# Computing the first three input-projection chunks side by side while x arrives, in a hybrid decoder layer

## The chip, the cores and the metric

One NeuronCore of one Trainium2 chip runs the whole layer as a single program. The metric is device time in microseconds for one execution; the kernel before took 484.26 us (median of 3 runs, 484.12 to 484.92).

## The reference, cut to what matters

```python
h = rmsnorm(x, norm_g)                       # x: 512 tokens x 1024
proj = jnp.einsum('bsd,de->bse', h, w_in)    # 1024 -> 4896 columns, split into 16 parts
# A: RG-LRU on lru_u:  conv (4 taps) -> xc;  r, i = sigmoid(xc @ wa + ba), sigmoid(xc @ wx + bx)
#    a = exp(-8 r softplus(-lam));  h_t = a h_{t-1} + sqrt(1 - a^2) i xc;  y = h * silu(z)
# B: native sparse attention (compressed, selected, window) with sigmoid gates, * silu(z)
# C: forgetting attention with a cumulative log-forget bias, * silu(z)
return x + jnp.einsum('bse,ed->bsd', concat(y_lru, y_nsa, y_fox), w_out)
```

Everything is float32. The mean of squares of x over the 1024 features gives one scale per token (rstd); the kernel multiplies it in after the projection, so the matmuls can start before it is known.

## The kernel before

**Precision.** Each float32 operand of the projections is split into a high part (a copy rounded to fp32r, made on ScalarE) and a low part (operand minus high, made on VectorE). A product is three matmuls: high x high, high x low, low x high.

**Tiling.** x arrives transposed as 8 slices of 128 features x 512 tokens (`x_raw`, 256 KB each), and becomes `xh` and `xl`. The input weights are cut into 39 chunks of 128 output columns (512 KB each); `CHUNKS` gives their order: u0 to u3 (chunks 0 to 3), fg (4), kc, vc, ks, kw (5 to 8), nq0 to nq3 (9 to 12), vn0 and vn1 (13, 14), zl0 to zl3 (15 to 18), and then the rest. A chunk lands in one of three `raw` slots; `split` (line 497, ScalarE) writes `wh`, `split_low` (line 763, VectorE) writes `wl`. `project(c)` (line 1074, TensorE) runs 8 x 3 matmuls of 128x512 (lines 1110 to 1112) into one of three PSUM banks. It waits for `wl_ready` of its chunk and, from the fourth chunk on, for the bank: the chunk three places back must have been read.

**The start.** SyncE issues x0, the channel constants, x1 to x3, w0, x4 to x7, w1, w2, constants, the compression weights, w3. ScalarE makes `xh` of each slice (line 634) and puts `split(0)` behind slice 4, `split(1)` behind slice 7, `split(2)` behind the square root (line 639). VectorE squares slices 0, 2, 4, 6, 7 (line 977) and makes `xl` of each (line 981); GpSimd squares slices 1, 3, 5 (line 462). TensorE sums all eight squares over partitions with a matrix of ones into MEAN (line 1253, a float32 matmul that the trace shows as two records), and only then begins `project(0)`. The scale is the square root on ScalarE and the reciprocal on VectorE (line 1004).

**The loop over chunks.** No scheduler: the order on each engine is the order of this code, and each engine's queue is served in order. In its turn c each engine does:
- TensorE: `project(c)`, then for the chunk before, if it is a u, the two gate matmuls `gates_of(c - 1)` (lines 1129 and 1130). So the gates of u3 stand behind chunk 4. The mean of squares of a normalised key or query chunk (line 1121) stands in the middle of the next chunk.
- ScalarE: `split(c + 3)`, `before(c)` (first conv tap of u, line 522; square of ks, line 534), then `after(c - 1)`: two sigmoids and a tanh of the gates (lines 544 to 547). At kc it also does a block that needs the tanh of all four u chunks (lines 661 to 669): four square roots, two small ones for the forget gate, four pairs of Ln and Exp, and only behind it `split(9)`.
- VectorE: `before(c)`: the eviction of chunk c times the scale (line 745) and three conv taps of u (line 756); `after(c - 1)`; pieces of the LRU tail at vc, ks, kw, nq0 and vn (lines 827 to 832, `TAIL_AT`), which need ScalarE's block; and last `split_low(c + 3)`.
- At vc, VectorE also needs the forget gate's logarithm from ScalarE's block (lines 798 and 799).

At zl0, TensorE's transpose (line 1165) needs the compressed-attention probabilities, which VectorE makes (line 897) after all that stands ahead of them in its queue.

Of the kernel before, what the change touches and what calls it, by code (L numbers as in the profile page):

```python
# [18 lines left out]
F32 = mybir.dt.float32  # L19
F32R = mybir.dt.float32r  # L20
BF16 = mybir.dt.bfloat16
ACT = mybir.ActivationFunctionType
ALU = mybir.AluOpType
AX = mybir.AxisListType

P = 128
SEQ, D = 512, 1024
HD = 64
KT = D // P
# [24 lines left out]
NSA_END = AT["zl", 3] + 1  # L54
# [29 lines left out]
TAIL_AT = (AT["vc", 0], AT["vc", 0], AT["ks", 0], AT["ks", 0], AT["kw", 0], AT["nq", 0], AT["vn", 0], AT["vn", 0])  # L84
OUT_ORDER = (2, 0, 3, 1)
STACK_LAG = 6
POOL_SQUARES = (1, 3, 5)
VECTOR_SQUARES = tuple(k for k in range(KT) if k not in POOL_SQUARES)

GAIN = {"ks": "ks_g", "kw": "kw_g", "nq": "nq_g", "fq": "fq_g", "fk": "fk_g"}  # L90

# [1 line left out]
def program(nc, xT, x_tok, w_in, w_out, chan, const, lru_w, cmp_w, out):  # L93
    ctx = ExitStack()
    with ctx:
        def sem(name):
            return ctx.enter_context(nc.semaphore(name))
# [98 lines left out]
        raw_loaded = [sem(f"raw_loaded{i}") for i in range(RAW)]  # L196
        wh_ready, wl_ready, w_used = sem("wh_ready"), sem("wl_ready"), sem("w_used")
        xh_ready, xl_ready, x_sq = sem("xh_ready"), sem("xl_ready"), sem("x_sq")
        x_sq_pool, x_sq_used = sem("x_sq_pool"), sem("x_sq_used")
        std_ready = sem("std_ready")  # L200
        rstd_ready, rstd_T, rcol_ready = sem("rstd_ready"), sem("rstd_T"), sem("rcol_ready")
        small_consts = sem("small_consts")
# [55 lines left out]

            return sum(0 if CHUNKS[x][0] in ("nq", "fq") else 4 for x in NORMED[:c])

        def pool_square(k):
            return (sq, work, std)[POOL_SQUARES.index(k)][:, :]

        def half_of(s):
            return slice(s * HD, (s + 1) * HD)
# [117 lines left out]
        @block.sync  # L383
        def _(sp):
            def load_w(c):
                if c >= N_STREAM:
                    return
                if c >= RAW:
                    sp.wait_ge(wl_ready, c - RAW + 1)
                src = w_in[c] if c < N_IN else w_out[c - N_IN]  # L390
                sp.dma_start(raw[:, c % RAW, :], src).then_inc(raw_loaded[c % RAW], 16)

            def stack(c):

                n = nth_normed(c)
                sp.wait_ge(h_ready, 2 * n + 2)
                sp.wait_ge(l_ready, n + 1)
                for s in range(2):
                    own, other = half_of(s), half_of(1 - s)
                    for plane in key_planes(c, s):  # L400
                        sp.dma_start(plane[other, :].bitcast(F32), plane[own, :].bitcast(F32)).then_inc(stacked, 16)

            def pair_up(i):

                sp.wait_ge(proj_read, proj_units(AT["kc" if i == 0 else "vc", 0]) + 1)
                if i == 1:
                    sp.wait_ge(kv_pe_ready, 1)
                for g in range(KVH):
                    half = slice(g * HD, (g + 1) * HD)
                    sp.dma_start(kv_pair[0:HD, g, :], kv_cm[half, i, :]).then_inc(kv_shifted[i], 16)  # L410
                    sp.dma_start(kv_pair[HD:P, g, 0:SEQ - 1], kv_cm[half, i, 1:SEQ]).then_inc(kv_shifted[i], 16)

            for k in range(KT):
                sp.dma_start(x_raw[:, k, :], xT[:, k, :]).then_inc(x_loaded[k], 16)
                if k == 0:
                    sp.dma_start(chn[:, :], chan).then_inc(chan_loaded, 16)
                if k == KT // 2 - 1:
                    load_w(0)
            load_w(1)
            load_w(2)  # L420
            sp.dma_start(cst[:, :], const).then_inc(const_loaded, 16)
            sp.dma_start(cmp_w_sb[:, :, :, :], cmp_w).then_inc(cmp_w_loaded, 16)
            load_w(3)
            sp.wait_ge(xl_ready, KT)
            sp.wait_ge(x_sq, len(VECTOR_SQUARES))
            sp.wait_ge(x_sq_pool, len(POOL_SQUARES))
            sp.dma_start(lru_w_sb[:, :, :, :], lru_w).then_inc(lru_w_loaded, 16)
            for c in range(4, N_STREAM + 6):
                load_w(c)
                k = c - 5  # L430
                if 0 <= k < N_IN:
                    if CHUNKS[k][0] in ("kc", "vc"):
                        pair_up(0 if CHUNKS[k][0] == "kc" else 1)
                k = c - STACK_LAG
                if 0 <= k < N_IN and CHUNKS[k][0] in ("ks", "kw", "fk"):
                    stack(k)
                if c == N_IN + 4:
                    sp.wait_ge(proj_done, proj_units(N_IN))
                    sp.dma_start(x_res[:, :, :], x_tok).then_inc(res_loaded, 16)
            for n, t in enumerate(OUT_ORDER):  # L440
                for half in range(2):
                    cols = slice(half * 512, (half + 1) * 512)
                    sp.wait_ge(out_ready, 2 * n + half + 1)
                    sp.dma_start(out[t * P:(t + 1) * P, cols], y_out[:, t, cols]).then_inc(stored, 16)
            sp.wait_ge(stored, 16 * 2 * NT)
# [3 lines left out]
        def _(pool):  # L449
# [7 lines left out]
            nc.gpsimd.memset(k_cmp[:, :, :], 0.0)  # L457
            nc.gpsimd.memset(v_cmp[:, :, :], 0.0)
            nc.gpsimd.memset(v_blocks[:, :, :], 0.0).then_inc(small_consts, 1)
            for k in POOL_SQUARES:  # L460
                pool.wait_ge(x_loaded[k], 16)
                nc.gpsimd.tensor_tensor(pool_square(k), x_raw[:, k, :], x_raw[:, k, :], ALU.mult).then_inc(x_sq_pool, 1)
            def scale_probs(first, last):
                for u in range(first, last):
                    group, h, b, t = unit(u)
# [28 lines left out]
        def _(act):  # L494
            link = chain(lambda: act, "act_chain")

            def split(c):
                if c >= N_STREAM:
                    return
                act.wait_ge(raw_loaded[c % RAW], 16 * (c // RAW + 1))  # L500
                wait_slot(act, c)
                act.activation(wh[:, c % HL, :], raw[:, c % RAW, :], ACT.Copy).then_inc(wh_ready, 1)  # L502

# [128 lines left out]
            for k in range(KT):  # L632
                act.wait_ge(x_loaded[k], 16)
                act.activation(xh[:, k, :], x_raw[:, k, :], ACT.Copy, scale=ch("norm_g", k)).then_inc(xh_ready, 1)
                if k == KT // 2:
                    split(0)
            split(1)
            act.wait_ge(x_sq_used, KT)
            act.activation(rstd_bc[:, :], MEAN[:, :], ACT.Sqrt, bias=eps1[:, :], scale=1.0 / D).then_inc(std_ready, 1)
            split(2)  # L640
            for c in range(NSA_END):
                if CHUNKS[c][0] == "zl":
                    t = CHUNKS[c][1]
# [2 lines left out]
                    act.activation(p, p, ACT.Exp).then_inc(cmp_exp, 1)  # L646
                if c >= 1:
                    norm_seeds(c - 1)
                split(c + AHEAD)
                before(c)  # L650
                read_tokens(c, 0, MIDDLE)
                if c >= 1:
# [56 lines left out]
        def _(dve):  # L709
# [260 lines left out]

            for k in range(KT):
                dve.wait_ge(x_loaded[k], 16)
                if k in VECTOR_SQUARES:
                    i = VECTOR_SQUARES.index(k)
                    if i >= 2:
                        dve.wait_ge(x_sq_used, VECTOR_SQUARES[i - 2] + 1)
                    dve.tensor_tensor(qr[:, i % 2, :], x_raw[:, k, :], x_raw[:, k, :], ALU.mult).then_inc(x_sq, 1)
                if k == 0:
                    dve.wait_ge(chan_loaded, 16)
                dve.wait_ge(xh_ready, k + 1)  # L980
                dve.scalar_tensor_tensor(xl[:, k, :], x_raw[:, k, :], ch("norm_g", k), xh[:, k, :].bitcast(F32),
                                         ALU.mult, ALU.subtract).then_inc(xl_ready, 1)
                if k == KT // 2 + 1:
                    split_low(0)
            split_low(1)

            dve.wait_ge(const_loaded, 16)
            dve.tensor_copy(ident_r[:, :], ident)
# [14 lines left out]
            dve.wait_ge(std_ready, 1)  # L1003
            dve.reciprocal(rstd_bc[:, :], rstd_bc[:, :]).then_inc(rstd_ready, 1)
            dve.wait_ge(rstd_ready, 1)
            split_low(2)
            for c in range(NSA_END):
                if CHUNKS[c][0] == "zl":
                    cmp_probs(CHUNKS[c][1])
                before(c)  # L1010

                if c == AT["kc", 0]:
                    dve.wait_ge(rstd_T, 1)
                    dve.tensor_copy(rstd_col[:, :], AUX_B[:, :].rearrange("p (t c) -> p t c", t=NT)[:, :, 0])\
                       .then_inc(rcol_ready, 1)
# [57 lines left out]
        def _(pe):  # L1073
            def project(c):
# [27 lines left out]
                for k in range(KT):  # L1102
                    if k == KT // 2 + 1 and c - 1 in NORMED:
                        head_mean(c - 1)
                    if k == KT // 2 and c == AT["zl", 0]:
                        cmp_scores(0)
                    if c == 0:
                        pe.wait_ge(xl_ready, k + 1)
                    hi, lo = wh[:, slot, k * P:k * P + m], wl[:, slot, k * P:k * P + m]
                    pe.matmul(dst, hi, xh[:, k, :], start=(k == 0), stop=False)  # L1110
                    pe.matmul(dst, hi, xl[:, k, :], start=False, stop=False)  # L1111
# [130 lines left out]


            pe.wait_ge(ones_ready, 1)
            for k in range(KT):
                if k in POOL_SQUARES:
                    pe.wait_ge(x_sq_pool, POOL_SQUARES.index(k) + 1)
                    square = pool_square(k)
                else:
                    i = VECTOR_SQUARES.index(k)  # L1250
                    pe.wait_ge(x_sq, i + 1)
                    square = qr[:, i % 2, :]
                pe.matmul(MEAN[:, :], ones[:, :], square, start=(k == 0),
                          stop=(k == KT - 1)).then_inc(x_sq_used, 1)
            for c in range(NSA_END):
                project(c)
                if c >= 1 and CHUNKS[c - 1][0] == "u":
                    gates_of(CHUNKS[c - 1][1])
                if c == AT["kc", 0]:
                    pe.wait_ge(rstd_ready, 1)  # L1260
                    pe.wait_ge(const_loaded, 16)
                    pe.wait_ge(lru_sig, 2 * LRU_T)
# [145 lines left out]
```

## Time and profile before

| | |
|---|---|
| median of 3 runs | 484.26 us |
| the profiled execution | 484.85 us, of which the recorded span is 483.0 us |
| TensorE matmul busy | 454.1 us (94%) |
| VectorE / ScalarE / GpSimd busy | 306.7 / 250.1 / 74.8 us |
| HBM read, written | 32.81 MB, 2.10 MB |

The chain of waits follows the work that ended last back to the start. A timeline row gives start, duration, engine, line, operation, output <- inputs, and in brackets the idle time before it and what ended it. Matmuls overlap: a 128x512 record lasts 0.40 us while the next starts 0.23 us after it, so the chain's pieces (0.23 us) are the rate to count with. PEclk is the granted TensorE clock as a share of 2.4 GHz.

### The profile page before, as it was taken

Reading aid. Unit: us, or ns where it says so; the run is one execution under the profiler, and the core shown is the slowest. Engines: PE = TensorE matmul, PEld = TensorE weight load, DVE = VectorE, ACT = ScalarE, POOL = GpSimd, SP = SyncE. Lnnn points to the kernel's source line nnn. Section 1 sums busy time; section 2 is a strip of 40 time slices with the busy share of each in tenths; the row PEclk is TensorE's granted clock in tenths of the full one; section 3 lists DMA queues with packets and bytes.
Section 4 is the critical chain, followed back from the end, with each engine's and each line's share of the span. In section 5 each row is a group of like instructions: output and inputs, shape, how many; then the busy total and the mean of one; then the engine's idle time right before and its main releaser. Section 6 shows DMA issues by size and latency. Waiting matters only on the chain.

```text
span 483.0 us, 6629 instructions
## 1 busy us (share of the span) xinstructions
PE 454.1 (94%) x2328; PEld 344.6 (71%) x2328; DVE 306.7 (63%) x560; ACT 250.1 (52%) x472; POOL 74.8 (15%) x121
## 2 busy tenths in 40 slices
PE   5899999999869989999999999999799996999997
PEld 1476688778758766667577897988666675788885
DVE  5976469887987876676427864757866358522204
ACT  4555684667454665666518864852565434312200
POOL 3001240000000155445400000000354300000000
PEclk9899999999979999999999999999899999899999
DMA  7722234431141200000011243552200002932004
GB/s 262 285 88 88 88 88 130 104 115 45 44 131 43 87 2 3 0 2 2 0 45 43 88 108 112 136 171 85 90 2 1 1 6 82 317 117 88 0 1 174
DMA packets 12960, 39.52 MB, mean 82 GB/s; under 512 B 1792, under 2 KB 2048, under 8 KB 12672
## 3 DMA queue, kind: packets, MB, share of 16 engines
q1 hardware_dynamic: 12928, 39.11, 25.0%
q8 instruction: 19, 0.31, 0.3%
q14 instruction: 13, 0.11, 0.1%
HBM read 32.81 MB, written 2.10 MB: 72 GB/s over the span
## 4 chain that ended last, share of the span: by engine, by line
PE 75%; DVE 14%; issue 4%; ACT 3%; POOL 2%; DMA 1%; SPq 0%; POOLq 0%; DVEq 0%; ACTq 0%
PE bank L1110 10%; PE bank L1112 10%; PE bank L1111 10%; PE bank L1224 6%; PE bank L1206 5%; PE bank L1324 4%; PE bank L1326 4%; PE bank L1325 4%; PE bank L1194 3%; PE bank L1198 3%; PE bank L1121 2%; DVE wl L767 2%; PE bank L1090 2%; PE bank L1140 2%; PE bank L1092 2%
## 5 line engine op out<-in xcount | busy, mean ns | idle before, releaser
L1110 PE MATMUL bank<-xh,wh 128*128 128x512 f32 (+1 forms) x264 | 112.4, 426 | 0.0
L1112 PE MATMUL bank<-xh,wl 128*128 128x512 f32 (+1 forms) x264 | 104.2, 395 | 0.0
L1111 PE MATMUL bank<-xl,wh 128*128 128x512 f32 (+1 forms) x264 | 103.8, 393 | 0.0
L767 DVE TENSOR_TENSOR wl<-raw,wh 128x1024 fp32r<-128x1024 f32 x51 | 62.0, 1220 | 33.9 <-ACT wh L502 33.5
L502 ACT ACTIVATE wh<-raw 128x1024 fp32r<-128x1024 f32 x51 | 53.1, 1049 | 34.9 <-PE bank L1326 34.6
L951 DVE TENSOR_REDUCE negmax<-bank 128x1 f32<-128x128 f32 (+3 forms) x96 | 46.1, 484 | 29.4 <-PE bank L1198 26.7
L1110 PEld LDWEIGHTS bank<-xh,wh 128*128 128x128 f32 (+1 forms) x264 | 49.7, 188 | 15.2 <-issue 5.0
L1111 PEld LDWEIGHTS bank<-xl,wh 128*128 128x128 f32 (+1 forms) x264 | 49.6, 188 | 14.6 <-issue 4.2
L1112 PEld LDWEIGHTS bank<-xh,wl 128*128 128x128 f32 (+1 forms) x264 | 49.4, 187 | 11.8
L610 ACT ACTIVATE probs<-bank,negmax 128x256 f32<-128x256 f32 (+3 forms) x77 | 40.5, 527 | 22.0 <-DVE negmax L951 20.6
L470 POOL TENSOR_SCALAR probs<-probs,rcp,gates 128x128 f32<-128x128 f32 (+3 forms) x52 | 31.7, 617 | 127.3 <-DVE rcp L965 126.8
L1324 PE MATMUL bank<-wh,yh 128*128 128x512 f32 x96 | 38.4, 400 | 4.3 <-DVE qr L745 4.3
L1325 PE MATMUL bank<-wl,yh 128*128 128x512 f32 x96 | 38.5, 401 | 0.0
L1326 PE MATMUL bank<-wh,yl 128*128 128x512 f32 x96 | 38.5, 401 | 0.0
L1206 PE MATMUL bank<-cst,probs 128*128 128x128 f32 x192 | 35.0, 280 | 2.9 <-POOL probs L470 2.3
L958 DVE COPY pT<-bank 128x128 f32<-128x128 f32 (+2 forms) x72 | 30.0, 416 | 2.0 <-PE bank L1206 1.5
L1090 PE MATMUL bank<-wh,xh 128*128 128x256 f32 x96 | 28.5, 297 | 1.4 <-ACT v_nsa L592 1.4
L1206 PEld LDWEIGHTS bank<-cst,probs 128*128 128x128 f32 x192 | 22.7, 142 | 8.8 <-POOL probs L470 6.8
L745 DVE TENSOR_TENSOR qr<-bank,rstd_bc 128x512 f32<-128x512 f32 (+1 forms) x23 | 15.8, 688 | 20.0 <-PE bank L1112 19.9
L1092 PE MATMUL bank<-wh,xl 128*128 128x256 f32 x96 | 26.9, 280 | 0.0
L1091 PE MATMUL bank<-wl,xh 128*128 128x256 f32 x96 | 26.9, 280 | 0.0
L1194 PE MATMUL bank<-kh_nsa,q_nsa 128*128 128x128 f32 (+3 forms) x64 | 25.6, 399 | 0.6 <-ACT probs L610 0.6
(200 smaller groups left out, 794.0 us busy)
## 6 DMA issues: line engine op xcount, KB each, us to landing
raw<-in_w_in SPq DMA_DIRECT2D x39, 512.0 KB, 3.3
raw<-in_w_out SPq DMA_DIRECT2D x12, 512.0 KB, 3.8
x_raw<-in_xT SPq DMA_DIRECT2D x8, 256.0 KB, 6.7
x_res<-in_x_tok SPq DMA_DIRECT2D x1, 2048.0 KB, 8.5
out_y<-y_out SPq DMA_DIRECT2D x8, 256.0 KB, 2.1
cmp_w_sb<-in_cmp_w SPq DMA_DIRECT2D x1, 1024.0 KB, 10.7
kh_fox<-kh_fox SPq DMA_DIRECT2D x8, 128.0 KB, 2.4
kl_fox<-kl_fox SPq DMA_DIRECT2D x8, 128.0 KB, 2.5
```

Of the source, the lines that this page charges most:

```text
L502: act.activation(wh[:, c % HL, :], raw[:, c % RAW, :], ACT.Copy).then_inc(wh_ready, 1)
L610: act.activation(probs_of(u, 0, n), SCORE[u % S_RING][:, 0:n], ACT.Exp, bias=negmax[:, u % M_RING:u % M_RING + 1], accum_out=rsum[:, q % R ...
L767: dve.tensor_tensor(wl[:, c % HL, :], raw[:, c % RAW, :], wh[:, c % HL, :].bitcast(F32), ALU.subtract).then_inc(wl_ready, 1)
L951: dve.tensor_reduce(negmax[:, s % M_RING:s % M_RING + 1], SCORE[s % S_RING][:, 0:n], AX.X, ALU.max, negate=True).then_inc(max_ready, 1)
L1110: pe.matmul(dst, hi, xh[:, k, :], start=(k == 0), stop=False)
L1111: pe.matmul(dst, hi, xl[:, k, :], start=False, stop=False)
L1112: mm = pe.matmul(dst, lo, xh[:, k, :], start=False, stop=(k == KT - 1))
L1194: pe.matmul(dst[:, 0:n], q, kh[:, 0:n], start=True, stop=False)
L1206: mm = pe.transpose(PT[u % PTB][:, cols], probs_of(u, j * P, (j + 1) * P), ident)
L1324: pe.matmul(dst, yh[:, e, toks], wh[:, c % HL, cols], start=(e == 0), stop=False)
L1325: pe.matmul(dst, yh[:, e, toks], wl[:, c % HL, cols], start=False, stop=False)
L1326: mm = pe.matmul(dst, yl[:, e, toks], wh[:, c % HL, cols], start=False, stop=(e == ET - 1))
```

## The change

- **Loads.** The first three chunks come as four slabs: slab i holds 256 of the 1024 columns of each of the three chunks (two feature slices), 384 KB in pieces of 1 KB. SyncE now issues x0, constants, slab 0, x1, x2, slab 1, x3, x4, slab 2, x5, x6, slab 3, x7, and the rest as it was.
- **Splits.** ScalarE makes the slab's high part behind `xh` of slices 0, 2, 4, 6, VectorE its low part behind `xl` of the same. `split(0)`, `split(1)`, `split(2)` and their low parts are gone. `split_low(3)` still stands behind turn 0 of VectorE's loop.
- **Squares.** VectorE squares the even slices, ScalarE the odd ones, GpSimd none.
- **TensorE.** `first_chunks` computes chunks 0, 1 and 2 together: for each slice k, three high x high, three high x low, three low x high. Squares are summed between the slices, the last one behind slice 4.
- **Gates.** With chunks 0 to 2 done together, the gates of u0 stand behind chunk 3, those of u1 in the middle of chunk 4 (fg), those of u2 behind chunk 4, those of u3 behind chunk 5 (kc).
- The transposes of the scale, and the copy of their result, move from kc to vc.

```diff
-POOL_SQUARES = (1, 3, 5)
-VECTOR_SQUARES = tuple(k for k in range(KT) if k not in POOL_SQUARES)
+FIRST = 3
+SLAB = 2
+SQUARES_BEHIND = ((1,), (2, 3), (4, 5), (6,), (7,), (), (), ())
+GATES_AT = ((AT["u", 3], False), (AT["fg", 0], True), (AT["fg", 0], False), (AT["kc", 0], False))
...
+            def load_slab(i):
+                src = w_in[0:FIRST, :, i * SLAB * P:(i + 1) * SLAB * P].rearrange("c p q -> p c q")
+                sp.dma_start(slab(raw, i), src).then_inc(slab_loaded[i], 16)
...
-                if k == KT // 2 - 1:
-                    load_w(0)
-            load_w(1)
-            load_w(2)
+                if k % SLAB == 0:
+                    load_slab(k // SLAB)
...
                 act.activation(xh[:, k, :], x_raw[:, k, :], ACT.Copy, scale=ch("norm_g", k)).then_inc(xh_ready, 1)
-                if k == KT // 2:
-                    split(0)
-            split(1)
+                if k % SLAB == 0:
+                    i = k // SLAB
+                    act.wait_ge(slab_loaded[i], 16)
+                    last = i == KT // SLAB - 1
+                    act.activation(slab(wh, i), slab(raw, i), ACT.Copy).then_inc(wh_ready if last else slab_high,
+                                                                               FIRST if last else 1)
+                else:
+                    act.activation(square_of(k), x_raw[:, k, :], ACT.Square).then_inc(x_sq_act, 1)
             act.wait_ge(x_sq_used, KT)
...
-            split(2)
...
+                if k % 2 == 0:
+                    dve.tensor_tensor(square_of(k), x_raw[:, k, :], x_raw[:, k, :], ALU.mult).then_inc(x_sq, 1)
...
+                if k % SLAB == 0:
...
+                    dve.tensor_tensor(slab(wl, i), slab(raw, i), slab(wh, i).bitcast(F32),
+                                      ALU.subtract).then_inc(wl_ready if last else slab_low, FIRST if last else 1)
...
-                if c == AT["kc", 0]:
+                if c == AT["vc", 0]:
                     dve.wait_ge(rstd_T, 1)
...
+            def first_chunks():
+                mean_square(0)
+                for k in range(KT):
...
+                    if k < KT - 1:
+                        for c in range(FIRST):
+                            pe.matmul(proj_bank(c)[:, :], wh[:, c, cols], xh[:, k, :], start=(k == 0), stop=False)
+                    pe.wait_ge(xl_ready, k + 1)
+                    if k < KT - 1:
+                        for c in range(FIRST):
+                            pe.matmul(proj_bank(c)[:, :], wh[:, c, cols], xl[:, k, :], start=False, stop=False)
...
+                    for c in range(FIRST):
+                        if k == KT - 1:
+                            pe.matmul(proj_bank(c)[:, :], wh[:, c, cols], xh[:, k, :], start=False, stop=False)
+                            pe.matmul(proj_bank(c)[:, :], wh[:, c, cols], xl[:, k, :], start=False, stop=False)
+                        mm = pe.matmul(proj_bank(c)[:, :], wl[:, c, cols], xh[:, k, :], start=False, stop=(k == KT - 1))
+                        if k == KT - 1:
+                            mm.then_inc(proj_done, 1)
+                    for x in SQUARES_BEHIND[k]:
+                        mean_square(x)
+
+            first_chunks()
+            for c in range(FIRST, NSA_END):
                 project(c)
-                if c >= 1 and CHUNKS[c - 1][0] == "u":
-                    gates_of(CHUNKS[c - 1][1])
-                if c == AT["kc", 0]:
+                for j, (at, middle) in enumerate(GATES_AT):
+                    if at == c and not middle:
+                        gates_of(j)
+                if c == AT["vc", 0]:
                     pe.wait_ge(rstd_ready, 1)
```

## Rows read from the trace of the kernel before

**Rows 1.** The page: busy time of TensorE, and the chain by engine.
```profile
PE 454.1 (94%) x2328; PEld 344.6 (71%) x2328; DVE 306.7 (63%) x560; ACT 250.1 (52%) x472; POOL 74.8 (15%) x121
...
PE 75%; DVE 14%; issue 4%; ACT 3%; POOL 2%; DMA 1%; SPq 0%; POOLq 0%; DVEq 0%; ACTq 0%
```

**Rows 2.** Waits of TensorE, 20 to 140 us: total, times, longest in us.
```profile
PE bank L1165 <- DVE qr L897: 4.8, 1, 4.8
```

**Rows 3.** Timeline of TensorE at the start: start, us, engine, line, operation.
```profile
4.60 2.05 PE L1253 MATMUL bank<-qr,ones 128*128 128x512 f32 x2 [4.60 <-DVE qr L977]
...
8.87 1.19 PE L1253 MATMUL bank<-qr,ones 128*128 128x512 f32 x2 [0.52 <-DVE qr L977]
```

**Rows 4.** Timeline of the other engines at the start.
```profile
5.15 1.04 POOL L462 TENSOR_TENSOR sq<-x_raw 128x512 f32<-128x512 f32 x1 [2.97 <-DMA x_raw<-in_xT]
...
8.12 1.38 ACT L634 ACTIVATE xh<-x_raw,chn 128x512 fp32r<-128x512 f32 x2 [2.19 <-DMA x_raw<-in_xT]
...
11.35 1.04 ACT L502 ACTIVATE wh<-raw 128x1024 fp32r<-128x1024 f32 x1
...
19.30 0.69 ACT L639 ACTIVATE rstd_bc<-bank,eps 128x512 f32<-128x512 f32 x1 [2.37 <-PE bank L1253]
...
20.32 3.33 DVE L1004 RECIPROCAL rstd_bc<-rstd_bc 128x512 f32<-128x512 f32 x1
```

**Rows 5.** The chain of waits on TensorE, 30 to 75 us: start, us, what.
```profile
30.29 0.23 PE bank L1112
30.52 0.86 PE bank L1129 x2
...
53.03 0.86 PE bank L1130 x2
...
65.35 0.39 PE bank L1269 x4
...
74.88 0.86 PE bank L1121 x2
```

**Rows 6.** Timeline of VectorE, 24 to 90 us.
```profile
24.96 0.69 DVE L745 TENSOR_TENSOR u_pad<-bank,rstd_bc 128x512 f32<-128x512 f32 x1
26.54 2.33 DVE L756 SCALAR_TENSOR_TENSOR xc<-u_pad,chn,xc 128x512 f32<-128x512 f32 x3 [0.89 <-ACT xc L522]
28.78 1.22 DVE L767 TENSOR_TENSOR wl<-raw,wh 128x1024 fp32r<-128x1024 f32 x1
...
65.38 0.69 DVE L745 TENSOR_TENSOR kv_cm<-bank,rstd_bc 128x512 f32<-128x512 f32 x1 [4.06 <-PE bank L1112]
...
71.42 1.20 DVE L767 TENSOR_TENSOR wl<-raw,wh 128x1024 fp32r<-128x1024 f32 x1
...
88.17 0.69 DVE L745 TENSOR_TENSOR qr<-bank,rstd_bc 128x512 f32<-128x512 f32 x1 [0.95 <-PE bank L1112]
```

**Rows 7.** Timeline of ScalarE, 53 to 74 us.
```profile
53.93 0.69 ACT L544 ACTIVATE tau<-bank,chn 128x512 f32<-128x512 f32 x1 [4.22 <-PE bank L1130]
...
69.36 1.99 ACT L502 ACTIVATE wh<-raw 128x1024 fp32r<-128x1024 f32 x2
73.26 0.63 ACT L534 ACTIVATE sq<-qr 128x512 f32<-128x512 f32 x1 [1.91 <-DVE qr L745]
```

**Rows 8.** Windows: stretch, length, busy us by engine, granted clock, DMA share, GB/s.
```profile
8.00:16.00 8.00, 4.90 (x10) 1.59 (x10) 7.82 (x9) 6.29 (x9) 2.18 (x2) 0.99 1.02 403
13.77:15.65 1.88, 0.00 (x1) 0.00 (x1) 1.88 (x4) 1.52 (x2) 0.00 (x0) 1.00 1.02 421
15.65:19.27 3.62, 3.62 (x5) 1.51 (x6) 3.55 (x9) 1.28 (x1) 0.00 (x0) 0.53 0.81 279
136.90:142.00 5.10, 5.08 (x21) 4.89 (x22) 4.78 (x10) 3.34 (x5) 0.00 (x0) 0.50 0.35 103
```

**Rows 9.** Timelines of VectorE and GpSimd around the third conv.
```profile
39.36 3.33 DVE L756 SCALAR_TENSOR_TENSOR xc<-u_pad,chn,xc 128x512 f32<-128x512 f32 x3 [0.88 <-ACT xc L522]
...
40.85 1.30 POOL L484 TENSOR_TENSOR ig<-ig,xc 128x512 f32<-128x512 f32 x1 [4.09 <-ACT ig L545]
```

More of the change, by code:

```diff
@@ L198, in program @@
         xh_ready, xl_ready, x_sq = sem("xh_ready"), sem("xl_ready"), sem("x_sq")
-        x_sq_pool, x_sq_used = sem("x_sq_pool"), sem("x_sq_used")
+        x_sq_act, x_sq_used = sem("x_sq_act"), sem("x_sq_used")
+        slab_loaded = [sem(f"slab_loaded{i}") for i in range(KT // SLAB)]
+        slab_high, slab_low = sem("slab_high"), sem("slab_low")
         std_ready = sem("std_ready")
@@ L259, in stack_copies, with square_of, slab @@
             return sum(0 if CHUNKS[x][0] in ("nq", "fq") else 4 for x in NORMED[:c])
-        def pool_square(k):
-            return (sq, work, std)[POOL_SQUARES.index(k)][:, :]
+        def square_of(k):
+            return y_lru[:, k // 2, :] if k % 2 else (qr[:, 0, :], qr[:, 1, :], sq[:, :], std[:, :])[k // 2]
+        def slab(x, i):
+            return x[:, 0:FIRST, i * SLAB * P:(i + 1) * SLAB * P]
         def half_of(s):
@@ L424, in _ @@
             sp.wait_ge(xl_ready, KT)
-            sp.wait_ge(x_sq, len(VECTOR_SQUARES))
-            sp.wait_ge(x_sq_pool, len(POOL_SQUARES))
+            sp.wait_ge(x_sq, KT // 2)
+            sp.wait_ge(x_sq_act, KT // 2)
             sp.dma_start(lru_w_sb[:, :, :, :], lru_w).then_inc(lru_w_loaded, 16)
@@ L459, in _ @@
             nc.gpsimd.memset(v_blocks[:, :, :], 0.0).then_inc(small_consts, 1)
-            for k in POOL_SQUARES:
-                pool.wait_ge(x_loaded[k], 16)
-                nc.gpsimd.tensor_tensor(pool_square(k), x_raw[:, k, :], x_raw[:, k, :], ALU.mult).then_inc(x_sq_pool, 1)
             def scale_probs(first, last):
@@ L499, in split @@
                     return
-                act.wait_ge(raw_loaded[c % RAW], 16 * (c // RAW + 1))
+                act.wait_ge(raw_loaded[c % RAW], 16 * (c // RAW))
                 wait_slot(act, c)
@@ L648, in _ @@
                     norm_seeds(c - 1)
-                split(c + AHEAD)
+                if c + AHEAD >= FIRST:
+                    split(c + AHEAD)
                 before(c)
@@ L972, in _ @@
                 dve.wait_ge(x_loaded[k], 16)
[L973 to L977, printed above, removed]
+                if k % 2 == 0:
+                    dve.tensor_tensor(square_of(k), x_raw[:, k, :], x_raw[:, k, :], ALU.mult).then_inc(x_sq, 1)
                 if k == 0:
@@ L982, in _ @@
                                          ALU.mult, ALU.subtract).then_inc(xl_ready, 1)
-                if k == KT // 2 + 1:
-                    split_low(0)
-            split_low(1)
+                if k % SLAB == 0:
+                    i = k // SLAB
+                    last = i == KT // SLAB - 1
+                    if last:
+                        dve.wait_ge(wh_ready, FIRST)
+                    else:
+                        dve.wait_ge(slab_high, i + 1)
+                    dve.tensor_tensor(slab(wl, i), slab(raw, i), slab(wh, i).bitcast(F32),
+                                      ALU.subtract).then_inc(wl_ready if last else slab_low, FIRST if last else 1)
             dve.wait_ge(const_loaded, 16)
@@ L1005, in _ @@
             dve.wait_ge(rstd_ready, 1)
-            split_low(2)
             for c in range(NSA_END):
@@ L1104, in project @@
                         head_mean(c - 1)
+                    if k == KT // 2 and (c, True) in GATES_AT:
+                        gates_of(GATES_AT.index((c, True)))
                     if k == KT // 2 and c == AT["zl", 0]:
                         cmp_scores(0)
-                    if c == 0:
-                        pe.wait_ge(xl_ready, k + 1)
                     hi, lo = wh[:, slot, k * P:k * P + m], wl[:, slot, k * P:k * P + m]
@@ L1244, in _, with mean_square @@
             pe.wait_ge(ones_ready, 1)
[L1245 to L1248, printed above, removed]
-                else:
[L1250 to L1253, printed above, removed]
+            def mean_square(k):
+                if k % 2 == 0:
+                    pe.wait_ge(x_sq, k // 2 + 1)
+                else:
+                    pe.wait_ge(x_sq_act, k // 2 + 1)
+                pe.matmul(MEAN[:, :], ones[:, :], square_of(k), start=(k == 0),
@@ L1254, in _ @@
                           stop=(k == KT - 1)).then_inc(x_sq_used, 1)
-            for c in range(NSA_END):
+            def first_chunks():
+                mean_square(0)
+                for k in range(KT):
+                    i = k // SLAB
+                    last = i == KT // SLAB - 1
+                    pe.wait_ge(xh_ready, k + 1)
+                    if last:
+                        pe.wait_ge(wh_ready, FIRST)
+                    else:
+                        pe.wait_ge(slab_high, i + 1)
+                    cols = slice(k * P, (k + 1) * P)
+                    if k < KT - 1:
[5 more added lines that the diff above has]
+                            pe.matmul(proj_bank(c)[:, :], wh[:, c, cols], xl[:, k, :], start=False, stop=False)
+                    if last:
+                        pe.wait_ge(wl_ready, FIRST)
+                    else:
+                        pe.wait_ge(slab_low, i + 1)
+                    for c in range(FIRST):
[7 more added lines that the diff above has]
+                        mean_square(x)
```

## The prediction

> **What bounds the kernel now.** I read the chain by engine first: 75% of it is TensorE, 14% VectorE [rows 1]. So time taken from TensorE counts, but not everywhere. The waits of TensorE between 20 and 140 us show where: it hardly waits until zl0, where it stands still for 4.8 us for VectorE's probabilities [rows 2]. A gain ahead of that place reaches the end only if VectorE arrives there earlier too. Followed back from it, VectorE has work without a pause longer than about 1 us to turn vc, which begins at 65.38 when TensorE hands over chunk vc [rows 6]. In it VectorE needs what ScalarE makes in its long block at kc: ScalarE starts on the gates of u3 at 53.93, as their matmuls end, and works without idling to `split(9)` at 69.36 [rows 5, 7]. `split(9)` is two instructions in 1.99, so the first is done at 70.4; VectorE takes it up at 71.42 [rows 6, 7]. ScalarE's path is thus 16.5 us long (53.9 to 70.4) and has 1.0 us to spare. Two ends meet at vc, and the change moves both.
>
> **The first phase.** x1 was there by 5.15 and x2 at 8.12 [rows 4]; in the new order slab 0 lies between them, so it lands between the two: I take 6.6. ScalarE rounds 1024 columns in 1.04 [rows 4], 768 in about 0.8: slice 0 starts on TensorE at 7.5 (6.0 to 9.0). From there TensorE has 72 matmuls at 0.233 (a chunk of 24 is 5.6) and seven sums of squares at 0.86, the size of a gate matmul of the same shape [rows 5]: 16.8 + 6.0 = 22.8. A sum of squares took 2.05 at 4.60 and 1.19 at 8.87 [rows 3], so the clock is at 1.2 GHz until about 9; of the 1.5 us before that half is lost: 0.75. The phase ends at 7.5 + 22.8 + 0.75 = 31.05, chunk 0 six matmuls earlier, at 29.65. Later slices don't hold it: with 400 GB/s from 8 us on [rows 8], the 3.7 MB up to x7 are in by about 16.5, and x7 is first wanted for its sum behind slice 4, near 24. Splits and squares on ScalarE (8 + 4 + 4 instructions of 0.55 to 0.8, about 10 us) and VectorE (about 12 us) fit into the same time. GpSimd's three squares were beside the path and free nothing. The square sums end near 24.8; square root and reciprocal follow in 4.4 as before (19.30 to 23.65 [rows 4]), at 29.2: just ahead of chunk 0.
>
> **A new wait behind it.** Chunk 3 needs `split_low(3)`, which stands in VectorE's queue behind the eviction of chunk 0 and its conv. Before, this was 7 us early. The eviction starts at 24.96, the low part at 28.78 and ends at 30.0: 5.05 us [rows 6]. Now it starts at 29.8, so chunk 3 starts at 34.9. TensorE idles 3.8 us, and behind it all gates are queued; nothing else is ready for it.
>
> **TensorE to the gates of u3.** Three chunks (16.8) and four pairs of gate matmuls (4 x 1.72 = 6.9) lie between: 58.6. ScalarE now sits on the gates of u0 (wait to 42.2) ahead of the conv of u2; by the same rows that conv is done at about 49.5, when TensorE wants it, and a GpSimd product beside a conv made it 1.0 longer (3.33 for 2.33 [rows 6, 9]). I add 0.3 (0 to 1.3). The gates of u3 end at 58.9; before at 53.89 [rows 5]: 5.0 late, though chunk 3 began earlier, because they stand one chunk further back and the stall is ahead of them.
>
> **ScalarE, then VectorE.** The block's 16.5 us run unchanged: `split(9)` is done at 75.4. Less the spare 1.0, `split_low(9)` and all that VectorE does behind it are 4.0 late. TensorE is also held: the mean of ks stood at 74.88, its square was ready at 73.89 [rows 5, 7], so it goes 3.0 late. VectorE waited 0.95 for TensorE at nq0 [rows 6]; with TensorE 3.2 late there (it restarts a little after the square), 3.2 of the 4.0 is left. From there to zl0 both queues keep their distances: **+3.2**.
>
> **Clock.** After 1.9 us without matmul work (13.77 to 15.65) the granted clock was at half, 1.2 GHz, for most of the next 3.6 us [rows 8]. The stall of 3.8 us should do the same to chunk 3: a stretch like that one costs 1.7, all on the path. **+1.7** (0 to 2.6: two stretches are seen from 136.9 to 142.0, behind the 4.8 us wait [rows 2, 8]). The wait of 3 us at the mean of ks may do it again: 1.2 if it does, taken as **+0.6**. The stretch at half clock behind zl0 is there before and after.
>
> **Moved or exchanged at no cost.** Transposes of the scale, kc to vc: 0.4 us of TensorE, same queue. The waits of SyncE on all squares lie ahead of the LRU weights, wanted at 40. w3 waits for the last slab's low part near 18, lands by 23 and is wanted at 34.
>
> **Sum.** 3.2 + 1.7 + 0.6 = **+5.5 us**. The profiled execution took 484.85, 0.6 above the median; I add to the median: 484.3 + 5.5 = **489.8**.
>
> **Rivals.**
> 1. *Faster: VectorE's path isn't held by ScalarE's block*, and the turn at vc still starts when TensorE hands it over. If chunk 3 then starts on TensorE's own pace (31.05 instead of 34.9), start to ks is 4.6 us shorter: 479.7. For it: in the trace vc began on a TensorE wait of 4.06 [rows 6]. Against it: the gates of u3 would end at 54.7, still 0.8 late, and the spare is 1.0. It decides only if the low part of chunk 3 is ready by 31 and the block is shorter than 16.5; 0.08.
> 2. *Given back exactly*: slab 0 at 5.15, clock up at once, no half-clock stretch. Chunk 3 starts at 33.5, 1.4 earlier, and 3.2 - 1.4 - 0.3 = +1.5, or with a further spare us nothing: 484.3 to 485.8; 0.12.
> 3. *Slabs land late.* They come in 1 KB pieces where the weights had 4 KB; no row prices one. Slab 0 at 10 instead of 6.6 moves slice 0 to 10.9; the 0.75 at low clock goes, a half-clock stretch may come after the gap behind the first sum: 3.4 - 0.75 + up to 1.7, so +8.2 to +9.9: 492.5 to 494. Against it: x0 and x1, in 2 KB pieces, were both there by 5.15 [rows 4], and the phase has slack for all slabs but the first; 0.10.
>    The Trainium skill's page "Perfetto Trace Analysis", section "DMA Optimizations", says that transfers under 2 KB carry a significant cost each, and also that splitting lets some work start sooner; the first speaks for this rival, the second for the change. No run here has shown 1 KB pieces yet.
> 4. *The forecast* (+1.5 to +8.5, the ends being the clock and conv terms at theirs): 0.70.
>
> **How the numbers follow.** Time 489.8. Low end: the forecast's lowest, 485.8, and half of rival 2: 485.0. High end: 3.2 + 2.6 + 1.2 + 1.0 = 8.0, plus 0.7 for slab 0 at 8.1: 493.0. Outside: rival 1, part of 2, most of 3, 2 in 10. This kernel's measurement tells about 0.2% (1.0 us) from no change. Faster by more: 0.08 (rival 1). Within: 0.08 (two thirds of rival 2). Slower: 0.84 (the rest).
>
> **What would show it.** Right: TensorE dense from 7.5 to 31; then idle about 3.8 us for `wl` of VectorE; PEclk below 1 behind it; the gates of u3 ending near 59 or later; ScalarE's four square roots near 64.5 (59.4 before); TensorE idle at the mean of ks; `split_low(9)` 4 us or more late; the 4.8 us wait at zl0 still there. Wrong: chunk 3 starting with no wait, or the probabilities at zl0 coming earlier than 136.9 although the gates of u3 are late.

## The result and the profile after

The changed kernel takes 495.6 us (median of 4 runs, 494.3 to 495.9) against 484.6 for the kernel before on the same chip: ratio 1.022, 95% interval 1.020 to 1.024. That is +11.0 us where +5.5 was forecast. The profiled execution took 494.31 with a span of 492.5, 9.5 more than the span of before, and is the fastest of the four runs; the rest of this section goes by it.

The start went as planned. TensorE's timeline begins with the first sum of squares and then slice 0 of the three chunks:

```profile
4.53 2.04 PE L1265 MATMUL bank<-qr,ones 128*128 128x512 f32 x2 [4.53 <-DVE qr L987]
...
6.15 1.70 PE L1282 MATMUL bank<-xh,wh 128*128 128x512 f32 x3
```

What TensorE waits for between 0 and 160 us (total, times, longest, in us) names the new waits. Three of the rows below were there before: the wait at zl0 (first row, 4.8 before [rows 2]), the one for the first square (4.5, 4.6 before) and the one for `v_nsa` (1.4 in both). The waits for `wl` (VectorE's low part of chunk 3), for the square of ks and for a conv are new:

```profile
PE bank L1180 <- DVE qr L910: 4.9, 1, 4.9
PE bank L1265 <- DVE qr L987: 4.5, 1, 4.5
PE bank L1125 <- DVE wl L780: 3.9, 1, 3.9
PE bank L1136 <- ACT sq L542: 3.6, 1, 3.6
PE bank L1105 <- ACT v_nsa L600: 1.4, 1, 1.4
PE bank L1144 <- DVE xc L769: 0.9, 1, 0.9
```

The chain of waits around the end of the three chunks (start, duration, what) goes from TensorE through the eviction of chunk 0, its conv and the low part of chunk 3, and back:

```profile
28.54 0.24 PE bank L1295
...
28.87 0.70 DVE u_pad L758
...
29.59 0.83 ACT xc L530
...
30.45 0.76 DVE xc L769
...
32.77 1.15 DVE wl L780
...
34.05 0.77 PE bank L1125
```

Further on, the gates of u3, ScalarE's block and `split_low(9)` answer to [rows 5], [rows 7] and [rows 6]. First the chain, then the timelines of ScalarE and VectorE:

```profile
60.71 0.87 PE bank L1145 x2
```
```profile
61.60 0.69 ACT L552 ACTIVATE tau<-bank,chn 128x512 f32<-128x512 f32 x1 [3.84 <-PE bank L1145]
...
67.12 2.20 ACT L674 ACTIVATE u_pad<-tau 128x512 f32<-128x512 f32 x4
...
77.05 1.99 ACT L510 ACTIVATE wh<-raw 128x1024 fp32r<-128x1024 f32 x2
```
```profile
67.11 0.69 DVE L758 TENSOR_TENSOR kv_cm<-bank,rstd_bc 128x512 f32<-128x512 f32 x1 [1.27 <-PE bank L1127]
...
72.06 0.70 DVE L811 TENSOR_SCALAR qr<-qr,chn 8x512 f32<-8x512 f32 x1 [3.87 <-ACT sq L677]
...
78.13 1.23 DVE L780 TENSOR_TENSOR wl<-raw,wh 128x1024 fp32r<-128x1024 f32 x1 [0.49 <-ACT wh L510]
...
95.71 0.69 DVE L758 TENSOR_TENSOR qr<-bank,rstd_bc 128x512 f32<-128x512 f32 x1 [1.75 <-PE bank L1127]
```

The block starts at 61.60 where it started at 53.93: 7.7 late. Chunk vc is handed over only 1.7 late (67.11, before 65.38), but VectorE now stands 3.87 in its turn for the forget gate's logarithm out of the block. `split_low(9)` is 6.7 late and now waits for ScalarE (0.49); the eviction of nq0 is 7.5 late and waits for TensorE (1.75, before 0.95). The transpose at zl0 comes at 144.47 instead of 136.92, also 7.55 late. From zl0 to the end another 2 us are lost. The windows (stretch, length, busy us by engine, clock, DMA share, GB/s) show the clock at half (1.2 GHz) behind three waits; of these the kernel before had only the last, and shorter:

```profile
34.00:39.30 5.30, 5.25 (x12) 4.18 (x13) 4.34 (x6) 0.82 (x1) 0.00 (x0) 0.50 0.31 102
39.40:42.20 2.80, 2.80 (x14) 2.29 (x13) 0.06 (x1) 0.00 (x0) 0.00 (x0) 1.00 0.59 187
80.40:83.70 3.30, 3.03 (x5) 1.80 (x6) 3.20 (x7) 1.10 (x3) 0.00 (x0) 0.50 0.35 76
144.50:151.90 7.40, 7.40 (x27) 6.63 (x28) 6.88 (x16) 5.17 (x6) 0.00 (x0) 0.50 0.21 74
```

Half a microsecond of TensorE is lost for each busy one at half clock: 2.7 of chunk 3, 1.5 behind the mean of ks, and 3.7 behind zl0 where it was 2.5 (136.9 to 142.0 [rows 8]). Further back a stretch near 420 is longer than in the kernel before, and one near 345 is gone.

So there are two candidates: the order of the queues (the low part of chunk 3, the gates, ScalarE's block), and the clock that falls where TensorE waits.

### The profile page after: what moved, and what is told of

Its sections match the earlier page's. It is cut to its first block, busy times and chain, and to the rows that moved or that the text cites. A ratio compares the mean times of both kernels' runs of the same rounds, so it can differ in the third digit from the quotient of the medians.

```text
span 492.5 us, 6640 instructions
## 1 busy us (share of the span) xinstructions
PE 457.3 (93%) x2328; PEld 348.0 (71%) x2328; DVE 303.7 (62%) x560; ACT 252.4 (51%) x477; POOL 70.7 (14%) x118
## 4 chain that ended last, share of the span: by engine, by line
PE 70%; DVE 15%; ACT 7%; issue 4%; POOL 2%; DMA 1%; POOLq 0%; DVEq 0%; ACTq 0%
PE bank L1125 8%; PE bank L1127 8%; PE bank L1126 8%; PE bank L1239 6%; PE bank L1221 5%; PE bank L1372 4%; PE bank L1374 4%; PE bank L1373 4%; PE bank L1209 3%; PE bank L1213 3%; PE bank L1136 2%; DVE wl L780 2%; PE bank L1265 2%; PE bank L1105 2%; PE bank L1155 2%
## 5 line engine op out<-in xcount | busy, mean ns | idle before, releaser
L1125 PE MATMUL bank<-xh,wh 128*128 128x512 f32 (+1 forms) x240 | 104.0, 433 | 3.9 <-DVE wl L780 3.9
L1127 PE MATMUL bank<-xh,wl 128*128 128x512 f32 (+1 forms) x240 | 96.2, 401 | 0.0
L1126 PE MATMUL bank<-xl,wh 128*128 128x512 f32 (+1 forms) x240 | 95.9, 399 | 0.0
L780 DVE TENSOR_TENSOR wl<-raw,wh 128x1024 fp32r<-128x1024 f32 x48 | 58.4, 1220 | 38.5 <-ACT wh L510 38.1
L510 ACT ACTIVATE wh<-raw 128x1024 fp32r<-128x1024 f32 x48 | 50.1, 1051 | 35.6 <-PE bank L1374 35.6
L1125 PEld LDWEIGHTS bank<-xh,wh 128*128 128x128 f32 (+1 forms) x240 | 46.2, 193 | 18.5 <-issue 9.1
L1126 PEld LDWEIGHTS bank<-xl,wh 128*128 128x128 f32 (+1 forms) x240 | 45.9, 191 | 13.7 <-issue 4.0
L1127 PEld LDWEIGHTS bank<-xh,wl 128*128 128x128 f32 (+1 forms) x240 | 45.8, 191 | 11.0
```

Of the source, the lines that this page charges most:

```text
L780: dve.tensor_tensor(wl[:, c % HL, :], raw[:, c % RAW, :], wh[:, c % HL, :].bitcast(F32), ALU.subtract).then_inc(wl_ready, 1)
L1127: mm = pe.matmul(dst, lo, xh[:, k, :], start=False, stop=(k == KT - 1))
```

## The experiments

Each time below is a median with the ratio to the kernel before on the same chip. The runs were taken on several chips, so a difference between two medians ("6.9 below") can be up to 0.9 us from the difference of the two ratios; where it matters both are given. "Low part early" is the edit of e1, "gates early" that of e5. The three sets of unread matmuls add work; they leave nothing out.

**e1: low part of chunk 3 early.**

```diff
+            split(3)
             act.wait_ge(x_sq_used, KT)
...
-                if c + AHEAD >= FIRST:
+                if c + AHEAD > FIRST:
                     split(c + AHEAD)
...
+            split_low(3)
             dve.wait_ge(x_sq_used, KT)
...
-                split_low(c + AHEAD)
+                if c + AHEAD > FIRST:
+                    split_low(c + AHEAD)
```

> The changed kernel, with the two splits of chunk 3 put ahead of the scale's square root and reciprocal, where ScalarE and VectorE idle; nothing else. Theory A (the forecast's path: wait for the low part of chunk 3, then gates of u3 one chunk further back, then ScalarE's block at kc, then VectorE to zl0): no wait ahead of chunk 3, which starts near 30 instead of 33.9; no half clock from 32.5 to 39.4; the conv of u2 still held behind the gates of u0, so the gates of u3 end at 54.7 to 55.7 (61.6 in the changed kernel, 53.9 before); time 484.3 to 486, so nearly the whole loss is gone and no gain is left. Rival B (the load phase with slabs and the new squares costs something that lasts): stays above 490. Rival C (TensorE's gain counts in full once the wait is gone): 480.

Measured: 488.7 (1.010, 1.007 to 1.012), 6.9 below the changed kernel (6.1 by the ratios). The wait fell to 0.5 us, there was no half clock at 34, ScalarE's block began at 55.1 and `split_low(9)` at 71.61: the path was back to within 0.2 us of [rows 6]. But 4 us of loss stayed. Most of the reason is in its windows: TensorE, now early, waits for the square of ks (3.6 us) and then runs at half clock for 6.7 us.

```profile
66.00:70.50 4.50, 4.50 (x20) 3.38 (x18) 4.29 (x7) 4.37 (x8) 0.00 (x0) 1.00 0.00 0
70.60:73.00 2.40, 0.00 (x0) 0.00 (x0) 1.93 (x3) 1.93 (x3) 0.00 (x0) 1.00 0.00 0
73.20:79.90 6.70, 5.74 (x11) 3.49 (x11) 6.56 (x11) 4.10 (x6) 0.00 (x0) 0.50 0.55 136
```

In VectorE's timeline of e1 the eviction of nq0 then waits for TensorE, 2.3 us later than at 88.17 [rows 6]:

```profile
90.43 0.69 DVE L759 TENSOR_TENSOR qr<-bank,rstd_bc 128x512 f32<-128x512 f32 x1 [2.73 <-PE bank L1130]
```

Theory A's path held, its time did not. Rival B (a lasting cost of the load phase) was still open.

**e6: e1, with the clock kept up at the mean of ks.**

```diff
+                        if c == AT["kw", 0]:
+                            for n in range(14):
+                                pe.matmul(NORM_W[:, :], xh[:, 0, 0:P], xh[:, n % KT, :], start=True, stop=True)
                         head_mean(c - 1)
```

> e1 with 14 matmuls of 128x512 whose result nobody reads ahead of the mean of ks, where TensorE idled 3.6 us and the clock fell to half from 73.1 to 80.0. Theory H (in e1 the path is whole again, and what is left of the loss, 4 us, is this half clock: chunk nq0 handed over 2.3 us late, and one more stretch later): no half clock there, time 485 to 486.5. Rival B (the new load phase has a cost that lasts): 488 to 489, as e1.

Measured: 486.4 (1.0036, 1.0016 to 1.0056), 2.3 below e1 (2.9 by the ratios). The same stretch at full clock:

```profile
73.20:79.90 6.70, 6.27 (x37) 4.67 (x36) 6.56 (x11) 4.11 (x6) 0.00 (x0) 1.00 0.54 130
```

Adding 14 useless matmuls saved 2.3 us. Its profiled span is 482.9, that of before 483.0, but these two aren't like for like: the mean granted clock over the execution was 0.986 in the one and 0.982 in the other. Of e6's ten runs the four at 0.986 took 484.1 to 485.3 and the six at 0.982 took 486.4 to 487.3; the kernel before has a median of 483.2 at 0.986 (10 runs) and 484.0 at 0.982 (22 runs). So at the same mean clock e6 is 1.6 to 2.5 us above before, and the ratio of all runs says 0.36%, 1.7 us, with an interval that excludes no difference. Rival B (a lasting cost of the load phase) is much smaller than the loss, but not excluded: what is left stays open.

**e2: the changed kernel, clock kept up behind the first three chunks.** 16 such matmuls stand behind `first_chunks()`.

> The changed kernel, with 16 matmuls of 128x512 whose result nobody reads put behind the first three chunks, 3.7 us of work where TensorE waits for the low part of chunk 3. They replace no work. Theory A: chunk 3 starts as before at 33.9 to 34.1, the clock stays at 2.4 GHz, the gates of u3 end 2.7 us earlier (58.9), and the half clock at the mean of ks may stay; time 2.7 to 4.5 below the changed kernel, 491 to 493. Rival D (the clock is the whole loss): 485. Rival E (the clock is beside the path): 495.

Measured: 492.7 (1.018, 1.015 to 1.021), 2.9 below the changed kernel (2.0 by the ratios). The clock is on the path, with about the size expected, and it isn't the whole loss. The half clock moved as well as went: the stretch at ks is 6.8 us long here (3.4 in the changed kernel), the one at zl0 6.8 instead of 10.2.

**e5: gates early, nothing else.**

```diff
-GATES_AT = ((AT["u", 3], False), (AT["fg", 0], True), (AT["fg", 0], False), (AT["kc", 0], False))
+GATES_AT = ((AT["u", 3], True), (AT["u", 3], False), (AT["fg", 0], True), (AT["fg", 0], False))
```

> The changed kernel with the gates alone moved (u0 in the middle of chunk 3, u1 behind it, u2 in the middle of fg, u3 behind fg); the low part of chunk 3 stays late. Theory A: chunk 3 still starts at 33.9 with the clock at half to 39.4; the gates of u3 end one chunk earlier, at 55.5 to 57 instead of 61.6, and as VectorE follows ScalarE's block with 1 us to spare, zl0 and the end come 4.5 to 6 earlier than in the changed kernel: 489.5 to 491. Rival F (the order of the gates is beside the path): 495.

Measured: 489.7 (1.012, 1.009 to 1.015), 5.9 below the changed kernel (5.1 by the ratios). ScalarE's block starts at 57.92 instead of 61.60:

```profile
57.92 0.69 ACT L552 ACTIVATE tau<-bank,chn 128x512 f32<-128x512 f32 x1 [2.49 <-PE bank L1145]
```

That is 3.7 earlier (TensorE waited 2.0 for convs in it). TensorE's wait for the square of ks is gone from its list, and with it the half clock at 80, but neither adds to the 3.7: the evictions of nq0 and zl0 are 3.6 earlier than in the changed kernel. The rest of the profiled gain of 5.8 comes behind zl0, from the clock: the half-clock stretch there is 3.4 us shorter (zl1 comes 4.95 earlier), and so is the one near 420 (1.1 more); one near 348, which the changed kernel doesn't have, takes 0.25 back. VectorE's turn at vc now begins on TensorE (68.91, after a wait of 3.67) and waits for ScalarE nowhere: with the gates early the other end of the path holds.

**e4: the kernel before, with the gates of u3 behind kc.**

```diff
-                if c >= 1 and CHUNKS[c - 1][0] == "u":
-                    gates_of(CHUNKS[c - 1][1])
-                if c == AT["kc", 0]:
+                if 1 <= c <= 3:
+                    gates_of(c - 1)
+                if c == AT["kc", 0]:
+                    gates_of(3)
+                if c == AT["vc", 0]:
                     pe.wait_ge(rstd_ready, 1)
```

> The kernel before, with one part of the change alone: the gates of u3 behind kc instead of behind fg, and with them the transposes of the scale behind vc. Theory A: the gates of u3 end at 61.1 instead of 53.9, 7.3 late; ScalarE's block has 1.0 to spare, so VectorE's low part of chunk 9 is 6.3 late and the time 4.5 to 6.3 longer, 489 to 491. Rival G (the block has more slack than the trace shows, and TensorE's own pace sets the end): 484.3 to 485.

Measured: 490.8 (1.014, 1.011 to 1.016). This one part of the change, put into the kernel before, costs 6.6 us (the profiled span grows by 6.5). The expectation's 61.1 was a slip (the gates of u3 were counted on top of their old place; one chunk back is 5.6, so 59.5), and ScalarE's timeline has 58.71 for the sigmoid behind them. Before, it was 53.93, and this kernel's first phase ran 0.65 earlier, so the shift is 5.4:

```profile
58.71 0.69 ACT L544 ACTIVATE tau<-bank,chn 128x512 f32<-128x512 f32 x1 [9.72 <-PE bank L1130]
...
75.20 1.23 DVE L767 TENSOR_TENSOR wl<-raw,wh 128x1024 fp32r<-128x1024 f32 x1 [0.49 <-ACT wh L502]
```

`split_low(9)` is 3.8 late (4.4 with the 0.65), so the 1.0 us of slack was read rightly. The end is later still. Here too TensorE waits 3.6 for the square of ks and the clock falls behind it, and the eviction of nq0 is 4.55 late; zl0 is 4.6 late. Behind zl0 the half-clock stretch is 3.4 us longer than in the kernel before (1.0 more lost), and so is the one near 420 (1.2 more); 0.35 comes back near 345, where a stretch is gone. So of the 6.5 about 4.6 is the path up to zl0, with the clock at ks in it, and 1.9 is the clock further back. The expected range was met by two errors that cancel: the slip, and the clock left out.

**e3: low part early and gates early.**

> As e1, and the gates of u0 in the middle of chunk 3, those of u1 behind chunk 3, of u2 in the middle of fg, of u3 behind fg. Theory A: the gates of u3 end at 48 to 50 instead of 53.9 before, ScalarE's block begins 4 to 6 us earlier, and with it everything to zl0; time 479 to 481, below both kernels. Rival F (VectorE's own load sets the time of zl0 whatever ScalarE's block does): 484 to 485.

Measured: 483.8 (0.9985, 0.9969 to 1.0001): the loss is gone, but the gain of 3 to 5 us isn't there. ScalarE's block begins at 52.5, not at 48 to 50. The chain shows why: with the gates early, the conv of u2 stands behind the sigmoids of u0 on ScalarE, the third tap of the convs of u2 and u3 takes 1.66 instead of 0.76, and TensorE waits for both.

```profile
36.35 1.28 ACT L552
37.64 0.69 ACT tau L552
38.33 0.59 ACT ig L553
...
40.61 0.72 ACT xc L530
...
42.93 1.66 DVE xc L770
...
48.79 1.67 DVE xc L770
...
50.50 1.12 PE bank L1147 x2
```

GpSimd's products of u1 and u2 begin at 42.54 and 48.41, beside the two long taps, as at 40.85 in [rows 9]. So the work of VectorE, ScalarE and GpSimd on the four u chunks bounds this stretch once TensorE does not. It reaches VectorE's turn at vc through TensorE, as in e5, and no longer through ScalarE's block:

```profile
63.51 0.69 DVE L759 TENSOR_TENSOR kv_cm<-bank,rstd_bc 128x512 f32<-128x512 f32 x1 [3.67 <-PE bank L1130]
```

Rival F named VectorE's load at zl0; it was its load here.

**e7 and e8: the clock at zl0.** 20 unread matmuls stand ahead of the transpose at zl0, in the kernel before (e7) and in e3 (e8).

```diff
+                    if t == 0:
+                        for n in range(20):
+                            pe.matmul(SCORE[1][:, :], xh[:, 0, 0:P], xh[:, n % KT, :], start=True, stop=True)
                     cmp_transpose(t)
```

> The kernel before with 20 matmuls of 128x512 whose result nobody reads at zl0, where TensorE idles 4.8 us ahead of the transpose and then runs at half clock from 136.9 to 142.0. If the clock there is on the path: 2 to 2.6 us less, 481.6 to 482.3. If VectorE sets the zl turns whatever the clock: 484.

> e3 (low part of chunk 3 early, gates early) with the same 20 matmuls at zl0 as e7. e3 and e7 touch different places, so their gains should add: 0.4 to 1.4 from e3 and 2 to 2.6 from the clock: 480 to 482, below the kernel before. If e7 shows nothing, 483.8.

Measured: e7 481.6 (0.9945, 0.9927 to 0.9963), e8 480.9 (0.9931, 0.9906 to 0.9957). The stretch that ran at 0.50 in [rows 8] runs at full clock in e7:

```profile
136.10:142.00 5.90, 5.72 (x34) 5.08 (x35) 5.73 (x12) 4.46 (x6) 0.00 (x0) 1.00 0.27 92
```

e8 is faster than both kernels, by 3 us than the one before and by about 14 than the changed one. Between e7 and e8 the intervals overlap: in time, what the side-by-side start adds can't be told from nothing. The profiled executions show what may lie behind that. The eviction of zl1 comes at 144.05 in e7 and at 142.54 in e8, and e8 is still 1.5 ahead at 335. Then the stretches at half clock near 340 and 410 are each twice as long in e8 (second pair) as in e7 (first pair), and 0.2 of the 1.5 is left at the end:

```profile
339.60:342.90 3.30, 3.30 (x14) 2.62 (x14) 2.44 (x7) 1.88 (x8) 1.92 (x4) 0.50 0.37 148
407.70:411.30 3.60, 3.45 (x8) 2.81 (x9) 2.11 (x4) 2.01 (x4) 0.00 (x0) 0.53 0.93 337
```
```profile
336.90:343.80 6.90, 5.81 (x20) 4.60 (x21) 4.98 (x14) 4.37 (x15) 2.92 (x5) 0.51 0.34 112
405.30:412.20 6.90, 5.47 (x13) 4.34 (x14) 5.40 (x8) 3.25 (x5) 0.00 (x0) 0.51 0.79 302
```

So in these two executions the side-by-side start, with both its edits, gained 1.5 us up to 335, and 1.3 of it went again with the clock; no run here holds the clock at those two places.

**e9: the changed kernel with the clock kept up at all three places.**

> The changed kernel with unread matmuls at all three places where TensorE waits: 16 behind the first three chunks, 14 ahead of the mean of ks, 20 at zl0; the queues are as in the changed kernel. With the clock held here and in e7, the difference of the two is what the order of the queues costs alone. Theory A: the gates of u3 end 5.1 to 6 later than in the kernel before, less 1.0 of slack and up to 1 at nq0: 3.2 to 5 us above e7, 485 to 487. If the queue order costs all of the loss: 492 or more. If the clock is all of it: 481 to 482.

Measured: 487.35 (1.0065, 1.0046 to 1.0084). Behind the start, no stretch at half clock is left ahead of 411 us. ScalarE's block starts at 59.48, in e7 at 53.28: 6.2 later; `split_low(9)` at 75.98 against 70.77: 5.2 later.

```profile
59.48 0.69 ACT L552 ACTIVATE tau<-bank,chn 128x512 f32<-128x512 f32 x1 [3.85 <-PE bank L1148]
```
```profile
53.28 0.69 ACT L544 ACTIVATE tau<-bank,chn 128x512 f32<-128x512 f32 x1 [4.22 <-PE bank L1130]
```

This splits the loss. With the clock held at these places in both (e9 against e7), what else differs costs 1.20% or 5.8 us: the order of the queues, and with it the load phase and whatever is left in e6. Holding the clock is worth 1.56% in the changed kernel (1.0221 less 1.0065) and 0.55% in the one before (1 less 0.9945): 4.9 us more. The two shares add up to the whole ratio by the way they are worked out, so their sum proves nothing. Nor is the split clean: near 411 e9 keeps a stretch at half clock of 6.8 us where e7 has one of 3.4 and another of 3.4 near 340. In the profiled executions the difference is 4.6 at zl0, 4.1 at 411 and 5.2 at the end, so some 0.6 of the 5.8 is the clock too. My estimate from these rows: about 5 us for the queues, and about 6 of the 11.0 for the clock.

## Why the prediction was right or wrong

- **What bounds the kernel**: right for the changed kernel. VectorE waits for ScalarE's block, and the block for the gates of u3; e4 and e5 moved the gates alone and the end followed, by 6.6 and 5.9 us, of which 4.6 and 3.6 stand in the profiles at zl0; the rest is the clock behind it. In e3 and e5 the other of the "two ends" holds: VectorE's turn at vc begins when TensorE hands it over, and nothing in it waits for ScalarE.
- **First phase**: right in kind, 1 us too long. I put slab 0 between x1 and x2, at 6.6, although SyncE issues it ahead of x1, and it was there by 5.2: ScalarE rounded it at once behind `xh`. x1 in turn came at 6.86 instead of 5.15. The matmuls ran slowly until about 9, as forecast; only their durations say so, for the profile's column of the granted clock reads 1.00 from 5 to 8 us in both kernels. The 1 KB pieces did no visible harm (393 GB/s from 8 to 16 us, 403 before); rival 3 fell. Of the Trainium skill's two sentences from "Perfetto Trace Analysis", "DMA Optimizations", the one on the cost of transfers under 2 KB is thus not borne out at this size; whether the splitting itself let work start sooner no run here shows, for none loads the same data unsplit.
- **Wait for the low part of chunk 3**: right. 3.9 us (forecast 3.8), chunk 3 at 34.0 (34.9).
- **Gates of u3**: forecast 58.9, measured 61.6; in e9, without the half clock, 59.5, which is 5.6 later than before (forecast 5.0) and 6.2 later than in e7, whose start was 0.65 earlier. The conv of u2 was the undersized term: 0.9 of waiting against the 0.3 taken, within its range of 0 to 1.3. The half clock in chunk 3 adds the other 2.1.
- **ScalarE to VectorE**: right, with 1.0 of slack (7.7 late at the block, 6.7 at `split_low(9)`). At nq0 I let VectorE win back 0.8; between e9 and e7 it won back 0.6. So the queues cost 4.6 at zl0, where 3.2 was forecast: the term had the right parts, with the gates 1.2 too early and the win-back 0.2 too large.
- **Clock**: the step that failed. Path and waits were right and both terms were too small, but this one missed most (about 6 us, where 2.3 was forecast) and left places out. I took 1.7 + 0.6 and set the stretch behind zl0 equal before and after. Measured: 2.7 behind the three chunks, 1.5 at the mean of ks, 1.2 more behind zl0, and 1.2 more in a stretch near 420 us that I hadn't looked at (0.3 came back near 345). The mistake is to price one stretch like one seen: stretches at half clock were 3.4, 6.8 or 10.2 us long in these traces, and later ones move when the program does. Together that is 6.3. The 4.9 by the ratios of e9 and e7 leaves out the last two, where neither kernel holds the clock: 5.4 without them. Why 4.9 and not 5.4 is not shown; slack on VectorE may take some.
- **Range**: 485.0 to 493.0, measured 495.6. With the high value of each term (3.2, 2.6, 1.2, 1.0 and 0.7 for slab 0) I had 8.7 us; what lay outside was the change at the later stretches (1.2, 1.2, less 0.3), which had no term at all. The low end of rival 4, +1.5, wasn't built from its terms either: with the clock and the conv at their lowest they give 2.9.
- **Rival 1** fell: in the changed kernel, and in e1, e2, e4, e6 and e9, where the gates of u3 stand behind kc, `split_low(9)` waits 0.5 for ScalarE. In the others, as in the kernel before, it doesn't. **Rival 2** had its first condition (slab 0 by 5.2), but not the clock. Its time was reached only by e3, once the queues were mended by hand: 483.8 (e1 took 488.7).

## What to carry to other kernels

When an edit frees the busiest engine early, write down for each other engine what stands in its queue behind the new hand-over: here one 1.2 us instruction behind an eviction and a conv, and a pair of matmuls one chunk further back, cost more than was freed (the first three chunks were done at 30.1 instead of 37.75, 1.7 of which were the gates that stood among them: 5.9 us). Price a stall of TensorE twice: once as the stall, once as the stretch at half clock behind it, and list every later place where such a stretch can lengthen. Where a stall couldn't be removed (3.9, 3.6 and 4.8 us here), matmuls that nobody reads saved 2.0 to 2.9 us at each of the three places where they were tried by themselves. Before you call a gain absent, look whether a later stretch at half clock swallowed it.

## What was not expected of the hardware

The same stall had different prices. 3.6 us of waiting for the square of ks was followed by a stretch of 6.8 us at 1.2 GHz in e1 and of 3.4 us in the changed kernel. Waiting 4.8 to 4.9 us at zl0 was followed by 6.8 us in the kernel before and by 10.2 in the changed one. And the matmuls became fast at different times at the start, with the same matmuls before them. Three low x high matmuls of slice 0 still took 1.38 at 9.68 in TensorE's timeline of e3 (first row), and 0.86 at 8.80 in that of the changed kernel (second):

```profile
9.68 1.38 PE L1298 MATMUL bank<-xh,wl 128*128 128x512 f32 x3
```
```profile
8.80 0.86 PE L1295 MATMUL bank<-xh,wl 128*128 128x512 f32 x3
```

Only that e3 started slice 0 0.8 later (6.99 against 6.15) tells them apart; whether that is the cause stays open. It bounds what can be told of this kernel from a single run: two runs of e3 differed by up to 2.7 us. In part the clock tells such runs apart. Of 44 runs of the kernel before, the 10 with a mean granted clock of 0.986 have a median of 483.2, the 22 at 0.982 one of 484.0, and the 12 at 0.979 one of 485.6.
